# Reordering four stages of a fused two-block transformer kernel: attention's mixing step, the MLP's column sums, a statistic in the gates, and the output projection's weight sums

## What is computed

```python
dk, dv, gk, gv, rest = projections of modulated x and ctx
s = einsum('bqhjd,bkhjd->bhjqk', dq, dk) * ATTN_SCALE          # two maps j for each differential head
p = softmax(s); a = p[:, :, 0] - lam * p[:, :, 1]; o_d = a @ dv
o_g = softmax(gq @ gk) @ gv                                     # grouped query attention
y_f = fft2(u_f).real
y_c = silu(layer_norm(depthwise_conv31(a * sigmoid(g)) + bias))
merged = g_f * (y_f @ w_f) + g_d * (o_d @ w_d) + g_g * (o_g @ w_g) + g_c * (y_c @ w_c)
x = x + gx1 * rms_norm(merged @ w_out, g_post_mix)
x = x + gx2 * rms_norm(square(relu(modulate(x) @ w_ff1)) @ w_ff2, g_post_mlp)
```

## Time and profile before

| | |
|---|---|
| Median of 3 runs | 3959.19 us (3953.01 to 3960.21) |
| The profiled execution | 3961.22 us, of it 3959.3 us span |
| Busy: PE, DVE, POOL, ACT | 94%, 47%, 26%, 21% |
| Read from HBM | 468.92 MB, 119 GB/s over the span |
| Mean granted clock of PE | 0.983 of full speed |

### The profile page before, as it was taken

How to read it: one execution, slowest core, us unless ns; L and a number is a source line. 1 busy time by engine, 2 the same in 40 slices (tenths; PEclk the granted TensorE clock), 3 DMA queues, 4 the chain that set the end, 5 groups by cost and what they waited for, 6 DMA issues and landing times. The chain is left out here.

```text
span 3959.3 us, 47929 instructions
## 1 busy us (share of the span) xinstructions
PE 3732.6 (94%) x18308; PEld 2556.1 (65%) x18308; DVE 1872.7 (47%) x3522; ACT 829.0 (21%) x1685; POOL 1013.0 (26%) x876
## 2 busy tenths in 40 slices
PE   8988779999999999999999999999999999999998
PEld 6876545555475577555554555555887767778887
DVE  3366232222322276887545566645125655143445
ACT  3124111111201265111212000002114611230001
POOL 1301200000023211223332223222142034443443
PEclk9989889999999999999999999999999999999999
DMA  5410499999611100222220332221110022212221
GB/s 213 185 70 12 158 356 394 395 392 391 243 59 44 47 2 11 80 86 97 80 100 23 121 123 107 107 85 54 48 67 31 12 66 85 84 64 96 85 85 54
DMA packets 72446, 476.18 MB, mean 120 GB/s; under 512 B 8288, under 2 KB 9696, under 8 KB 18976
## 3 DMA queue, kind: packets, MB, share of 16 engines
q1 hardware_dynamic: 69008, 462.40, 31.2%
q0 software_dynamic: 2640, 8.65, 0.8%
q10 hardware_dynamic: 576, 2.10, 0.1%
HBM read 468.92 MB, written 4.19 MB: 119 GB/s over the span
## 5 line engine op out<-in xcount | busy, mean ns | idle before, releaser
L1030 PE MATMUL ps<-projected,weight_ring 128*128 128x384 f32 (+1 forms) x672 | 245.8, 521 | 0.0
L3575 PE MATMUL ps<-projected,weight_ring 128*128 128x384 f32 (+1 forms) x768 | 223.0, 434 | 1.2 <-DVE mlp_u L3774 0.7
L2472 DVE SCALAR_TENSOR_TENSOR sb_x_all<-ps,sb_modulation_ada,sb_x_all 128x512 f32<-128x512 f32 x144 | 106.5, 750 | 245.9 <-PE ps L2297 216.3
L1030 PEld LDWEIGHTS ps<-projected,weight_ring 128*128 128x128 f32 x672 | 127.7, 190 | 106.1 <-issue 45.9
L3575 PEld LDWEIGHTS ps<-projected,weight_ring 128*128 128x128 f32 x768 | 144.8, 190 | 62.5 <-issue 3.0
L3575 PE MATMUL ps<-projected,mlp_weight_sums 128*128 128x384 f32 x480 | 166.1, 489 | 0.0
L3575 PE MATMUL ps<-h2b,weight_ring 128*128 128x384 f32 (+1 forms) x512 | 153.4, 444 | 6.5 <-ACT h2b L943 6.5
L2995 DVE SCALAR_TENSOR_TENSOR projected<-projected,sb_vectors 128x497 f32<-128x497 f32 (+26 forms) x270 | 157.8, 649 | 1.6
L2132 POOL DMA_INDIRECT h<-tokens,own_tokens x31 | 31.1, 1003 | 488.0 <-PE ps L2268 429.4
L2855 PE MATMUL ps<-projected,gate_sums 128*128 128x384 f32 (+1 forms) x512 | 150.2, 437 | 5.0 <-POOL gate_sums L3135 5.0
L1446 DVE TENSOR_REDUCE attention_shift<-ps 128x1 f32<-128x768 f32 (+1 forms) x160 | 130.6, 844 | 47.8 <-PE ps L1316 47.8
(11 more groups left out here) (671 smaller groups left out, 7680.1 us busy)
## 6 DMA issues: line engine op xcount, KB each, us to landing
weight_ring<-w_stream SPq DMA_DIRECT2D x217, 1024.0 KB, 5.0
expert_weights<-w_moe SPq DMA_DIRECT2D x125, 1024.0 KB, 23.0
weight_ring<-w_moe SPq DMA_DIRECT2D x40, 1024.0 KB, 23.7
h2b<-w_moe SPq DMA_DIRECT2D x33, 1024.0 KB, 23.1
weight_ring<-w_stream SPq DMA_DIRECT2D x16, 512.0 KB, 3.8
weight_ring<-w_stream SPq DMA_DIRECT2D x16, 384.0 KB, 3.3
sb_x_all<-xT SPq DMA_DIRECT2D x4, 768.0 KB, 6.9
tokens<-h_tokens ACTq DMA_DIRECT2D x4, 512.0 KB, 9.9
```

The costliest lines, as they stand in the source:

```text
L1030: ins = nc.tensor.matmul(core.ps[:, 2 * slot + half, 0:n], w_of(k), h_of(k)[:, a:a + n], start=(first and k == 0), stop=(last and k == chu ...
L2472: v.scalar_tensor_tensor(core.x[:, k, NCTX:T], ps[:, bank, :], core.mods["ada"][:, 40 + k, 1:2], core.x[:, k, NCTX:T], ALU.mult, ALU.add). ...
L3575: ins = nc.tensor.matmul(acc, wq[:, k, :], bq[:, k, :], start=(first and k == 0), stop=(last and k == 3), skip_group_check=True)
```

## The change

Four parts.

1. MLP. The third column sum of the hidden values is issued in the first down unit, behind u2, and no longer with the first two. `whole` also takes the modulation unit behind the first down unit of groups 0 to 2 (numbers 3, 11 and 19 of the 24).
2. Attention. For a differential pair DVE runs reciprocal and ratio, then the scaling of pair p-3, then the mix. For the other pairs nothing changes.
3. First output projection. POOL makes the four weight sums of its first unit at the start of the windowed attention phase, in the 256 context columns of `core.x`, which hold nothing then; the first unit of the projection reads them there.
4. Gates, unit 9. The first half of the statistic moves from behind z1 to behind x2, the second from behind y2 to behind z2; DVE's second mean moves behind c12.

```diff
@@ attention_phase
         @block.gpsimd
         def _(pool):
+            if side is not None:
+                side_quarters(pool, side, core.stream.arrived(pool, 0), side_ready)
             for p in range(N):
...
+            def mix(p):
+                keys, b, r = pairs[p]["keys"], 2 * (p % 2), p % 2
+                if pairs[p]["diff"]:
                     dve.wait_ge(ratio_ready, mixes[p])
                     nc.vector.scalar_tensor_tensor(prob[:, b, 0:keys], prob[:, b + 1, 0:keys], ratio[:, r:r + 1],
                                                    prob[:, b, 0:keys], ALU.mult, ALU.add).then_inc(mixed, 1)
...
+                ahead = 0 <= p - 1 < N and pairs[p - 1]["diff"]
+                if ahead:
+                    inverse(p - 1)
                 if p >= 3:
                     scale(p - 3)
-                if 0 <= p - 1 < N:
+                if ahead:
+                    mix(p - 1)
+                elif 0 <= p - 1 < N:
                     inverse(p - 1)
@@ gates_phase, PE
                 product(z, s[:, 0], right(0, 1), True, False)
-                if j == TAPPED:
-                    if bg:
-                        pe.wait_ge(bg.added, bg.n_turn)
-                    pe.wait_ge(tapped, 1)
-                    statistic(acc, 0)
...
                 product(x, q.a12(w), right(4, 0), False, True)
+                if j == TAPPED:
+                    if bg:
+                        pe.wait_ge(bg.added, bg.n_turn)
+                    pe.wait_ge(tapped, 1)
+                    statistic(acc, 0)
                 pe.wait_ge(u2_out, j + 1)
                 pe.wait_ge(t_ready, 2)
                 product(y, s[:, 2], th[:, 1], False, False)
-                if j == TAPPED:
-                    pe.wait_ge(mean_out, 1)
-                    statistic(acc, 1)
...
                 product(z, s[:, 3], right(4, 1), False, True)
+                if j == TAPPED:
+                    pe.wait_ge(mean_out, 1)
+                    statistic(acc, 1)
@@ gates_phase, DVE
-                if j == TAPPED:
-                    mean_half(1)
                 dve.wait_ge(products, 7 * j + 6)
                 dve.wait_ge(u2_out, j + 1)
                 nc.vector.tensor_tensor(quarter(0, 1), z, quarter(0, 1), ALU.add).then_inc(c12_out, 1)
+                if j == TAPPED:
+                    mean_half(1)
@@ new
+def side_quarters(pool, x, w, ready):
+    def part(quarter):
+        return quarter(w).rearrange("p (d e) m -> p d e m", d=2)
+    q = Quarters
+    s = [SideQuarter(x, i).whole() for i in range(4)]
+    pool.tensor_tensor(s[0], part(q.a21), part(q.a22), ALU.add).then_inc(ready, 1)
+    pool.tensor_tensor(s[2], part(q.a11), part(q.a21), ALU.subtract).then_inc(ready, 1)
+    pool.wait_ge(ready, 1)
+    pool.tensor_tensor(s[1], s[0], part(q.a11), ALU.subtract).then_inc(ready, 1)
+    pool.wait_ge(ready, 3)
+    pool.tensor_tensor(s[3], part(q.a12), s[1], ALU.subtract)
@@ seven_phase
-                s = sw[:, i % 2]
+                s = [sw[:, i % 2, r] for r in range(4)]
+                if side is not None and i == 0:
+                    s = [SideQuarter(side, r) for r in range(4)]
@@ mlp_phase
-        whole = [i for i in range(len(mods)) if i == 0 or (i + 1) % (2 * U) == U - 1]
+        whole = [i for i in range(len(mods)) if i == 0 or (i + 1) % (2 * U) in (U - 1, U)]
...
                 v.tensor_tensor(t[:, 1], t[:, 0], b11, ALU.subtract).then_inc(ready, 1)
+                yield
                 v.tensor_tensor(t[:, 2], b21, t[:, 0], ALU.subtract).then_inc(ready, 1)
...
                 v.tensor_tensor(u2[:, p, :], y, m1[:, p, :], ALU.add).then_inc(u2_ready, 1)
+                if not up and j == 0:
+                    next(hid_sums)
@@ first_block
-            attention_phase(core, "window", pairs, masked=mask, y=cat)
+            attention_phase(core, "window", pairs, masked=mask, y=cat, side=core.x)
...
-                        mods=mod_units("mod0", 2, 8), burst=2)
+                        mods=mod_units("mod0", 2, 8), burst=2, made=1, side=core.x)
```

More of the change, by code:

```diff
@@ L1208, in _, with attention_phase @@
             add(n - 1)
-def attention_phase(core, name, pairs, masked=None, neg_lambda=None, y=None):
+def attention_phase(core, name, pairs, masked=None, neg_lambda=None, y=None, side=None):
     nc, ps = core.nc, core.ps
@@ L1247, in attention_phase @@
         sink_set, keys_masked = (ph.sem("sink_set"), ph.sem("keys_masked")) if sink else (None, None)
+        side_ready = ph.sem("side_sums_ready") if side is not None else None
         if y is not None:
@@ L1449, in inverse @@
             def inverse(p):
-                keys, b, r = pairs[p]["keys"], 2 * (p % 2), p % 2
+                b, r = 2 * (p % 2), p % 2
                 dve.wait_ge(p_ready, 2 * p + 2)
@@ L3137, in weight_quarters, with __init__, __getitem__, whole @@
     pool.tensor_tensor(s[:, 3], q.a12(w), s[:, 1], ALU.subtract).then_inc(ready, 1)
+class SideQuarter:
+    def __init__(self, x, i):
+        self.x, self.i = x, i
+    def __getitem__(self, at):
+        p, k, _ = at
+        return self.x[p, 2 * self.i + k // 2, k % 2 * P:(k % 2 + 1) * P]
+    def whole(self):
+        return self.x[:, 2 * self.i:2 * self.i + 2, 0:2 * P].rearrange("p d (e m) -> p d e m", m=P)
+def side_quarters(pool, x, w, ready):
[9 more added lines that the diff above has]
+    pool.tensor_tensor(s[3], part(q.a12), s[1], ALU.subtract)
 def column_quarters(dve, b, lo, n, t, ready, made):
@@ L3275, in seven_phase @@
 def seven_phase(core, name, b, lo, n, units, th=None, conv=None, mods=(), burst=0, heads=None, tail=None,
-                sw=None, made=0, ahead=None):
+                sw=None, made=0, ahead=None, side=None):
     nc, ps, stream = core.nc, core.ps, core.stream
@@ L3380, in _ @@
                     pe.wait_ge(c12_out, i - 1)
-                product(z, s[:, 0], right(0, 1), True, False)
+                product(z, s[0], right(0, 1), True, False)
                 if kq and len(kq.turns.get(i, ())) == 2:
@@ L3389, in _ @@
                     pe.wait_ge(c21_out, i - 1)
-                product(y, s[:, 1], th[:, 0], True, False)
+                product(y, s[1], th[:, 0], True, False)
                 if kq and len(kq.turns.get(i, ())) == 1:
@@ L3398, in _ @@
                 pe.wait_ge(t_ready, 3)
-                product(y, s[:, 2], th[:, 1], False, False)
+                product(y, s[2], th[:, 1], False, False)
                 if kq:
@@ L3403, in _ @@
                 sums(i, 4)
-                product(z, s[:, 3], right(4, 1), False, True)
+                product(z, s[3], right(4, 1), False, True)
                 if kq:
@@ L3742, in _ @@
                 jn.normal(dve, j, KD - 1)
+            next(h_sums)
             next(h_sums)
```

## The result

| | before | after |
|---|---|---|
| Median of 5 runs | 3960.21 us (3953.01 to 3964.35) | 3935.73 us (3932.63 to 3937.55) |
| The profiled execution, its span | 3961.22 us, 3959.3 us | 3935.73 us, 3933.9 us |
| Ratio after / before, 95% interval | | 0.9934 (0.9924 to 0.9945) |
| Busy PE, DVE, POOL | 94%, 47%, 26% | 95%, 47%, 26% |
| Mean granted clock of PE | 0.983 | 0.983 |

The change makes the kernel 24.5 us faster by the medians, 25.4 us by the spans. The forecast was 3932 us, 27 us faster than the median it started from (3959.19 us).

What follows compares the result with a forecast made beforehand. PE, busy 94%, was taken to bound the kernel, with the gaps in its work. Terms -4.4 - 4.6 - 12.1 - 4.4 - 0.4 = -25.9 us, -27 with half the slow product, gave 3932 us; range 3922 to 3945.

Steps and rivals of the forecast that it cites:

- attention: Differential pairs, both layers: with only the scaling between value product and mix, the mix starts sooner; -12.1 us, bounds 0 and 17.7.
- projection: First output projection: PE's waits for POOL's first and third weight sums go, 4.4 us; the moved sums cost 0.
- slow product: First output projection, product behind PE's second wait for POOL: 3.61 us where the same shape took 1.99; 1.6 us extra.
- MLP, layer 0: First down units: waits for u2 go, 6.7 us, less 2.3 us for three modulation units on PE; net -4.4 us.
- MLP, layer 1: First down units: PE's waits for the sum u2 go, -4.6 us, bounds -4 and -5.
- gates: Moved statistic exchanges PE's wait for one on ACT's copy: layer 0 gains 1.1 us, layer 1 loses 0.7; net -0.4.
- the wait for the mix: PE's waits for the mixing of two probability maps in attention: 14.0 us in 37 waits, to become about 2 to 4.
- both lines of u2: PE's waits for the MLP sum u2, 6.1 us in layer 0 and 4.0 in layer 1: both gone.
- the short pairs: Attention, six differential pairs of 256 keys, which wait longer (0.65 us): each gains the full 0.41 us, 2.5 in sum.
- The eight first pairs: Attention, eight pairs without DVE idle time before the scaling: 0.1 us each; by the skill's DRAIN rule, nothing.
- Rival C: Attention: exponentials ending 2.5 us later than seen delay scaling and PE's value product; 0.7 us late gives 3985 us; chance 0.03.
- Rival B: Products that ran slow after a wait run fast everywhere once waits are gone: 3922 to 3927 us; chance 0.07.

Runs made afterwards that it cites:

- The split alone: Kernel before with only the MLP's third column sum moved behind u2, modulation units left as they were: 3947.63 us, ratio 0.9964.

## Why the prediction was right, term by term

| term, us | forecast | read in the stages |
|---|---|---|
| attention | -12.1 | -11.5 (means of the kernels; -13.4 between the two profiles) |
| projection | -4.4, slow product 1.6 by half | -6.3 |
| MLP, layer 0 | -4.4 | -4.3 at the full clock, -6.0 against before |
| MLP, layer 1 | -4.6 | -5.0 |
| gates | -0.4 | -0.5 at the full clock, +1.2 against before |

The signs named for each step came: the wait for the mix at 1.4 us (2 to 4 forecast), both lines of u2 gone, POOL's four sums ahead of the first spread, ACT's copy in the gates with 2.25 and 0.97 us (2 and 1 forecast).

**Attention** held in its detail. From one pair's spread product to the next, PE took 4.30, 4.30, 4.14 and 4.14 us in the four differential pairs of a tile before, and 4.19, 3.93, 3.76 and 3.77 after; the plain pairs kept 4.41, 4.40, 4.68 and 4.67. So three in four gained 0.37 us where 0.40 was forecast, the first of a tile 0.11 us where 0.1 was. Of the short pairs I had 0.41 us each; they gained 0.46 to 0.72, 3.2 us in place of 2.5; why, no run here separates. The first pair of 768 keys behind the short ones became 0.26 us longer (3.43 to 3.69), which the forecast did not have. The eight first pairs settle what the Trainium skill was weighed for (VectorE: DVE Perf Modes, "The DRAIN you can't avoid"), by which they gain nothing. From reciprocal to mix took 0.50 us before (1411.02 to 1411.52, scaling ahead of it at 1410.81) and 0.58 after with the scaling inside (1431.04 to 1431.62), so the four starts span 0.58 us in place of 0.71. The trace speaks against the rule as I read it, by 0.13 us a pair. The same section adds that a next operation that is not held back starts earlier, and the prediction left that out: the scaling started 0.19 us behind the ratio (1431.23 to 1431.42), the mix, which waits for the ratio, 0.31 us behind it where nothing stood between (1411.21 to 1411.52).

```profile
1411.02 0.15 DVE L1455 RECIPROCAL attention_inverse<-attention_sums 128x2 f32<-128x2 f32 x1
1411.21 0.27 DVE L1458 TENSOR_SCALAR attention_ratio<-attention_inverse,attention_sums,neg_lambda 128x1 f32<-128x1 f32 x1
1411.52 1.02 DVE L1461 SCALAR_TENSOR_TENSOR attention_prob<-attention_prob,attention_ratio 128x768 f32<-128x768 f32 x1
...
1431.04 0.15 DVE L1458 RECIPROCAL attention_inverse<-attention_sums 128x2 f32<-128x2 f32 x1
1431.23 0.27 DVE L1461 TENSOR_SCALAR attention_ratio<-attention_inverse,attention_sums,neg_lambda 128x1 f32<-128x1 f32 x1
1431.42 0.28 DVE L1482 TENSOR_TENSOR projected<-ps,attention_prob_t 128x128 f32<-128x128 f32 x1
1431.62 1.01 DVE L1468 SCALAR_TENSOR_TENSOR attention_prob<-attention_prob,attention_ratio 128x768 f32<-128x768 f32 x1
```

**Projection.** Both waits went and nothing took their place; DVE's column sums were not late. The term that was mis-sized is the slow product, which I counted by half. All six kernels with the wait show it, so it belonged to the sum in full: -6.0, measured -6.3. The moved sums took 1.26 us each, not 2.2.

**MLP.** The size was right and the reading incomplete: I costed the two edits as one and did not see that either removes the waits of layer 0 alone. The split alone gave -5.9 (580.7 against 586.6 us).

**Gates.** The exchange of waits was foreseen, and layer 1 (+0.77, forecast +0.7) too. In layer 0 the unit is 0.45 us longer between the two profiles, where 1.1 us less was forecast: the forecast took the product behind the new wait at 2.6 us, and it took 4.54. That is the clock and not the order. With the old order the low clock fell behind the wait of 3.29 us in three kernels of six, as here in the kernel with the attention part alone:

```profile
1835.29 3.15 PE L2871 MATMUL ps<-projected,sb_ones 128*128 128x384 f32 x6 [3.30 <-DVE sb_modulation_mod L478]
1838.23 3.53 PE L2864 MATMUL ps<-projected,gate_sums 128*128 128x384 f32 x8
```

Like compared with like, the new order gains 1.24 us at the full clock and 1.0 us at the low one (table of the stages), near the 1.1 us of the forecast. What the forecast lacked is a price for the low clock on either side, although the profile of before had a slow product behind a wait of 2.41 us. That this profile ran at the full clock behind its 3.29 us, and the profile after the change did not behind its 2.25, I take as chance: nothing that the runs vary explains it.

**The sum.** At the full clock the parts give -11.5 - 6.3 - 4.3 - 5.0 - 0.5 = -27.6 us, where -27 was forecast and the medians gave -24.5 (by the interval of the ratio, -22 to -30, so the 3.7 us between 3932 and 3935.73 are within the scatter). Between the two profiled executions, window and projection are shorter by 6.3 us, attention by 7.4 and 6.1, the MLP by 6.1 and 4.8, and the gates longer by 1.2: -29.4 us, and the span fell by 25.4. The 4.0 us between lie where nothing was changed, 3.4 of them behind two waits that the kernel before had too, each at the same length. First before, then after:

```profile
2036.80 2.82 PE L3355 MATMUL ps<-merged,weight_ring 128*128 128x384 f32 x8 [2.06 <-PEq L258]
3473.43 1.97 PE L3355 MATMUL ps<-merged,weight_ring 128*128 128x256 f32 x8 [2.41 <-PEq L258]
```

```profile
2023.13 4.28 PE L3398 MATMUL ps<-merged,weight_ring 128*128 128x384 f32 x8 [2.05 <-PEq L258]
3451.10 3.65 PE L3398 MATMUL ps<-merged,weight_ring 128*128 128x256 f32 x8 [2.42 <-PEq L258]
3452.00:3454.00 2.00, 2.00 (x6) 1.56 (x5) 1.93 (x3) 0.00 (x0) 0.00 (x0) 0.50 0.92 266
```

4.28 us in place of 2.82, and 3.65 in place of 1.97. The last line is the window 3452 to 3454 (us, busy and instructions of PE, its weight loads, DVE, ACT, POOL, then the granted clock, the share of DMA, GB/s): the clock is 0.50, the lower of the two levels, 1.2 GHz. Over a whole execution the low clock is granted for about as long in both (1 minus the granted clock, summed over all windows of 2 us, is 66.2 us before and 67.3 us after), but the same sum runs from 65.4 to 77.5 us in the thirteen profiles, and it counts stretches in which PE had little to do.

Rival C, late exponentials, did not show: PE's wait of its scores for them was 3.7 us before and is 2.9 after, in two waits. It was not forced in an experiment, so its threshold stays an estimate. Rival B, slow products that run fast once their wait is gone, came true in the changed stages (projection and MLP of layer 0, 1.6 and 1.7 us); in this profile slow products at unchanged places took as much away.

## What to carry to other kernels

Look for what is queued ahead of the operation that the critical engine waits for, and ask of each item when its own reader needs it; an item with a late reader goes behind. When two edits aim at one wait, price each alone, since the second may only add its cost. Before moving a consumer behind the next piece of work, look at the input of that piece: here the best place was the gap in front of the next wait.

## What the runs showed of the hardware

Behind some waits of PE the granted clock falls to its lower level (0.50), and whether it does differs at one and the same wait from one profiled execution to the next. Counted over the thirteen profiled kernels, one execution of each:

| wait of PE, us | place | low clock behind it |
|---|---|---|
| 1.93 to 1.96 | u2, MLP of layer 0 | 3 of 12 |
| 2.05 to 2.06 | first product of the output projection, layer 0, near 2030 | 9 of 13 |
| 2.24 to 2.59 | ACT's copy, gates of layer 0 | 4 of 5 |
| 2.41 to 2.42 | first product of the output projection, layer 1, near 3460 | 8 of 13 |
| 2.41 to 2.42 | POOL's third sum, first output projection | 6 of 6 |
| 3.29 to 3.30 | modulation sum, gates of layer 0 | 3 of 6 |

The product behind the wait of 2.05 us took 2.82 us in four kernels and 4.24 to 5.46 in nine. Behind ACT's copy it took 4.39 to 4.54 us in four kernels and this in the fifth:

```profile
1841.57 2.85 PE L2871 MATMUL ps<-h2b,weight_ring 128*128 128x384 f32 x8 [2.25 <-ACT gates_sigmoid L2962]
```

So a stage with such a wait is worth up to 1.7 us more or less in one trace (588.3 against 586.6 us in the MLP, 24.93 against 23.44 in the gates), and a single profile can't price it. Where the waits went, no low clock was seen again: not in the projection's first unit in seven kernels, not in the MLP of layer 0 in nine. Whether a wait removed lowers the low clock of the whole execution, the profiles don't show.

POOL's sum of 128x512 took 1.26 us with DVE on PSUM beside it, and 2.2 us in the projection beside DVE's column sums. DVE pays too. Its last column sum there took 2.28 us before, with POOL's sums beside it, and 1.22 us after the change, without them:

```profile
403.11 2.28 DVE L3151 TENSOR_TENSOR project_out_h_sums<-mixed,project_out_h_sums 128x1024 f32<-128x1024 f32 x1
```

```profile
401.88 1.22 DVE L3192 TENSOR_TENSOR project_out_h_sums<-mixed,project_out_h_sums 128x1024 f32<-128x1024 f32 x1
```

DVE's column sum of 128x1536 took 2.44 us in its new place, with a sum of POOL running from 2210.04, and 1.74 us in the kernel with the split alone, where it ran clear of POOL (2225.05). A moved operation on one of these engines can lengthen one on the other.
